# Three of 31 convolution steps moved to GpSimd, and four projection rows moved earlier, in the first mixer of a two-layer hybrid block

## The reference, cut to what matters

```python
u = h @ w_in                                        # h: 768 tokens (256 context, 512 latent) x 1024
a = u[..., :CONV_W] * jax.nn.sigmoid(u[..., CONV_W:2 * CONV_W])
bp = u[..., 2 * CONV_W:]
a = dwconv(a, w_dw, b_dw, (15, 15))                 # depthwise, 31 steps; latent rows of 64 tokens apart
a = jax.nn.silu(layernorm(a, ln_g, ln_b))
pooled = stack([centred_mean(bp[g], w) - bp[g] for g, w in enumerate((2, 4, 8, 16))])
p = (einsum('...gc,gcd->...gd', pooled, w_pool) + b_pool) * pool_scale
y = concatenate([a, p], axis=-1) @ w_out            # 2048 rows of w_out: 1024 for a, 1024 for p
```

## Time and profile before

| | |
|---|---|
| median of 3 runs | 2470.08 us |
| the profiled execution | 2473.15 us, of which the span from first to last instruction is 2471.5 us |
| busy in the span | PE 2326.1 us (94%), DVE 1627.3 (66%), ACT 946.7 (38%), POOL 430.7 (17%) |
| mean granted TensorE clock | 0.969 of full speed |
| chain that ended last | PE 78%, DMA 12%, DVE 4% |
| DVE, line 2491 | 232 instructions, 241.1 us |

### The profile page before, as it was taken

The page is one execution under the profiler, slowest core; times in us unless marked ns, Lnnn a source line. Parts: engine busy times, 40 slices in busy tenths (PEclk is TensorE's granted clock), DMA queues, the critical chain, the costliest instruction groups (busy, mean ns, idle before and its releaser), DMA issues.

```text
span 2471.5 us, 42712 instructions
## 1 busy us (share of the span) xinstructions
PE 2326.1 (94%) x16387; PEld 1555.0 (63%) x16388; DVE 1627.3 (66%) x2005; ACT 946.7 (38%) x1167; POOL 430.7 (17%) x461
## 2 busy tenths in 40 slices
PE   5999989998999999999979999999999799999984
PEld 2555534457788888888857887666645455555542
DVE  2799985447888888888876651677534533454544
ACT  3000014115777777777754232466421111111111
POOL 0533531220000000000020000211000223233322
PEclk9999989999999999999979999999998899999997
DMA  9102075529999999999992133212533989999997
GB/s 340 57 33 70 34 287 167 185 112 400 421 422 394 393 388 383 386 391 388 354 353 81 60 126 109 79 56 77 194 147 158 389 319 373 402 421 420 419 420 295
DMA packets 154320, 649.12 MB, mean 263 GB/s; under 512 B 27866, under 2 KB 42874, under 8 KB 99458
## 3 DMA queue, kind: packets, MB, share of 16 engines
q1 hardware_dynamic: 126912, 578.45, 59.5%
q0 software_dynamic: 16192, 57.53, 6.4%
q10 hardware_dynamic: 11138, 12.07, 1.4%
HBM read 595.13 MB, written 52.86 MB: 262 GB/s over the span
## 4 chain that ended last, share of the span: by engine, by line
PE 78%; DMA 12%; DVE 4%; issue 2%; ACT 2%; POOL 1%; SPq 1%; DVEq 0%; ACTq 0%; POOLq 0%
PE ps L968 75%; DMA arena<-in_w_dram 6%; DMA xs_d<-arena 2%; DMA chunk<-in_w_ada_dram 1%; DVE arena L2369 1%; PE ps L1210 1%; ACT arena L1614 1%; PE ps L1188 1%; PE ps L1194 1%; DMA wx<-in_w_dram 1%; DMA arena<-h_d,uix 1%; PE ps L1057 0%; POOL arena L767 0%; DMA buf_d<-arena 0%; DVE arena L2146 0%
## 5 line engine op out<-in xcount | busy, mean ns | idle before, releaser
L968 PE MATMUL ps<-arena 128*32 128x256 f32 (+5 forms) x10296 | 1192.7, 409 | 37.7 <-ACT arena L1614 10.9
L968 PEld LDWEIGHTS ps<-arena 128*32 128x32 f32 (+1 forms) x10296 | 652.8, 130 | 523.8 <-issue 320.7
L2422 DVE TENSOR_TENSOR wl<-wx,wh 128x2048 fp32r<-128x2048 f32 x228 | 511.5, 2285 | 25.2 <-ACT wh L1614 25.2
L1614 ACT ACTIVATE arena<-ps 128x256 f32<-128x256 f32 (+5 forms) x389 | 176.6, 478 | 863.4 <-PE ps L968 624.9
L1614 ACT ACTIVATE wh<-wx 128x2048 fp32r<-128x2048 f32 x228 | 432.6, 1915 | 85.1 <-PE ps L968 73.0
L2369 DVE COPY arena<-arena 128x2048 f32<-128x2048 f32 x180 | 222.8, 1297 | 274.0 <-PE ps L968 231.7
L968 PE MATMUL ps<-wh,xT 128*128 128x512 f32 x1184 | 380.4, 395 | 6.6 <-DVE xT L2428 4.2
L968 PEld LDWEIGHTS ps<-wh,xT 128*128 128x128 f32 x1184 | 223.2, 188 | 59.2 <-DVE xT L2428 4.6
L2491 DVE SCALAR_TENSOR_TENSOR arena<-arena,par 128x768 f32<-128x768 f32 x232 | 241.1, 1112 | 0.0
L968 PE MATMUL ps<-wl,xT 128*128 128x512 f32 x608 | 239.9, 395 | 0.0
L968 PE MATMUL ps<-wh,gT 128*128 128x512 f32 x608 | 199.5, 399 | 0.0
(11 more groups left out here) (362 smaller groups left out, 2270.5 us busy)
## 6 DMA issues: line engine op xcount, KB each, us to landing
wx<-in_w_dram SPq DMA_DIRECT2D x228, 1024.0 KB, 8.6
arena<-in_w_dram SPq DMA_DIRECT2D x192, 1024.0 KB
arena<-in_w_ada_dram SPq DMA_DIRECT2D x40, 1024.0 KB, 8.8
craw<-in_w_in_c_dram SPq DMA_DIRECT2D x8, 2048.0 KB, 9.0
buf_d<-arena POOLq DMA_DIRECT2D x1, 14848.0 KB, 57.3
arena<-buf_d POOLq DMA_DIRECT2D x19, 512.0 KB, 10.7
buf_d<-arena POOLq DMA_DIRECT2D x19, 512.0 KB, 7.9
arena<-in_w_in_ab_dram SPq DMA_DIRECT2D x8, 1024.0 KB, 12.5
```

Of the source, the lines that this page charges most:

```text
L968: return pe.matmul(bank_ap, lhsT, rhs, start=first, stop=last)
L1614: return act.activation(out_, in_, f, **kw)
L2422: v.tensor_tensor(wl[:, g], wx[:, g], whs[g % NH].bitcast(F32), ALU.subtract).then_inc(m["low"], 1)
```

## The change

For each tile, POOL takes the last three steps of the convolution (28, 29 and 30), after its pooling work for the tile of the same number and after DVE has laid out the padded input: three tensor_scalar and two adds of 768 elements, into an accumulator `gacc`. DVE does 28 steps, adds its two accumulators, waits for POOL, and adds `gacc`. The four rows of `pooled_half(1, ...)` that stood between the two `group_sums` are taken out one by one into the list, as steps h0 to h3. They need banks 6 and 7 for themselves from h0 on, so p5 to p7 use banks 1 and 2, and the modulation vectors 0 to 2 share bank 0, for which slices s4 and s8 wait until ACT has copied the vector before.

```diff
+        gacc = [at(o, S) for o in (6144 + 12 * S, 6144 + 13 * S) * 3 + (49616, 49616 + S)]
...
                 assert n == POOL_DONE[p]
+                pool.wait_ge(conv_s, CONV_OPS * p + 2)
+                acc = gacc[p].rearrange("p (r w) -> p r w", w=GRID_W)
+                for k in range(VTAPS, TAPS):
+                    src, w = apad[p % 2][:, :, k:k + GRID_W], par[:, p, k:k + 1]
+                    if k == VTAPS:
+                        step(pool.tensor_scalar(acc, src, w, None, ALU.mult))
+                    else:
+                        part = at(40912, ROWS, GRID_W)
+                        step(pool.tensor_scalar(part, src, w, None, ALU.mult))
+                        step(pool.tensor_tensor(acc, acc, part, ALU.add))
...
                 if kind == "mods":
+                    if i in (4, 8):
+                        pe.wait_ge(u_ev, i // 4)
                     mods(i)
+                    continue
+                if kind == "half":
+                    for half in range(2):
+                        pe.wait_ge(wo_in[2 * half + 1], 16)
+                    pe.wait_ge(p_rdy, i + 1)
+                    pooled_half(1, lambda k, t: catT[:, k, t * P:(t + 1) * P], wo, KD + i, KD + i + 1)
                     continue
...
             group_sums(lambda ct: catT[:, ct, :], range(4))
-            pooled_half(1, mixed, wo, KD, KD + 4)
             pe.wait_ge(conv_s, CONV_OPS * KD)
...
                 if kind == "pooled":
                     act.wait_ge(pg_mm, i + 1)
+                    if i in (4, 5):
+                        act.wait_ge(conv_s, CONV_OPS * (i + 1))
...
-                for k in range(TAPS):
+                for k in range(VTAPS):
...
-                v.wait_ge(conv_s, CONV_OPS * ct + 2 + TAPS)
+                v.wait_ge(conv_s, CONV_OPS * ct + 2 + VTAPS)
                 v.tensor_tensor(acc[0], acc[0], acc[1], ALU.add).then_inc(conv_s, 1)
+                v.wait_ge(conv_s, CONV_OPS * ct + 3 + VTAPS)
+                v.wait_ge(pool_s, POOL_DONE[ct] + GTAPS)
+                v.tensor_tensor(catT[:, ct, :], catT[:, ct, :], gacc[ct], ALU.add).then_inc(conv_s, 1)
...
-VBANK = (0, 1, 2, 3, 0, 2, 0, 6, 0, 2)
+VBANK = (0, 0, 0, 3, 0, 2, 0, 6, 0, 2)
+VCOL = (0, 256, 0, 0, 0, 0, 0, 0, 0, 0)
...
-CONV_OPS = 2 + TAPS + 1
+VTAPS = 28
+GTAPS = 2 * (TAPS - VTAPS) - 1
+CONV_OPS = 2 + VTAPS + 2
...
-              "s0 s1 p5 s2 s3 s4 s5 s6 p6 s7 s8 s9 p7 s10 s11").split():
+              "s0 s1 p5 s2 s3 h0 h1 s4 s5 s6 h2 p6 s7 h3 s8 s9 p7 s10 s11").split():
```

More of the change, by code:

```diff
@@ L369, in vector_ps @@
         def vector_ps(w, c):
-            return ps[32 * c:32 * c + 2, VBANK[w], 0:UW]
+            o = VCOL[w]
+            return ps[32 * c:32 * c + 2, VBANK[w], o:o + UW]
         vstage = [at(o, UW) for o in (1024, 2048, 3072, 43120, 36976, 37232, 29696, 49520, 48256, 50432)]
@@ L1403, in _ @@
                     pe.wait_ge(pool_s, POOL_DONE[2 * g + 1])
-                    wide(3072, lambda k: wpool[:, 2 * g + k, q * P:(q + 1) * P],
+                    wide(pooled_at(i), lambda k: wpool[:, 2 * g + k, q * P:(q + 1) * P],
                          lambda k: pooled[(2 * g + k) % 4], 2).then_inc(pg_mm, 1)
@@ L1630, in vector_out @@
                 act.wait_ge(u_mm, 4 * w + 4)
-                go(vstage[w], ps[:, VBANK[w], 0:UW], ACT.Copy).then_inc(u_ev, 1)
+                go(vstage[w], ps[:, VBANK[w], VCOL[w]:VCOL[w] + UW], ACT.Copy).then_inc(u_ev, 1)
                 if ST_OF[w] is not None and w != 6:
@@ L1891, in _ @@
                     act.wait_ge(pg_mm, i + 1)
-                    go(catT[:, KD + i, :], psf[:, 3072:3072 + S], ACT.Identity,
+                    if i in (4, 5):
+                        act.wait_ge(conv_s, CONV_OPS * (i + 1))
+                    b0 = pooled_at(i)
+                    go(catT[:, KD + i, :], psf[:, b0:b0 + S], ACT.Identity,
                        scale=par[:, i, TAPS + 4:TAPS + 5], bias=pscb[:, i:i + 1]).then_inc(p_rdy, 1)
@@ L2726, in x_sem, with pooled_at @@
     return x_place(n, j) % 3
+def pooled_at(i):
+    return 512 if i >= 5 else 3072
 def lg_before(n, t):
@@ L2830 @@
 for _p in range(KD):
-    POOL_DONE.append((POOL_DONE[-1] if _p else 0) + (2 * (_p // 2 + 1) + 4 if _p < 6 else 11))
+    POOL_DONE.append((POOL_DONE[-1] + GTAPS if _p else 0) + (2 * (_p // 2 + 1) + 4 if _p < 6 else 11))
 AB_ORDER, _last = [], None
 for _step in ("V0 G0 P0 V1 G1 P1 V2 G2 P2 V3 p0 G3 P3 V4 p1 G4 P4 V5 G5 P5 V6 p2 G6 p3 V7 P6 G7 p4 P7 "
-              "s0 s1 p5 s2 s3 s4 s5 s6 p6 s7 s8 s9 p7 s10 s11").split():
-    _kind = {"V": "value", "G": "gate", "P": "pool", "p": "pooled", "s": "mods"}[_step[0]]
+              "s0 s1 p5 s2 s3 h0 h1 s4 s5 s6 h2 p6 s7 h3 s8 s9 p7 s10 s11").split():
+    _kind = {"V": "value", "G": "gate", "P": "pool", "p": "pooled", "s": "mods", "h": "half"}[_step[0]]
     AB_ORDER.append((_kind, int(_step[1:]), _last))
```

## The result

The changed kernel takes 2512.42 us (median of 3 runs, 2511.96 to 2513.47) against 2470.08, +42.3 us by the medians. The ratio of the two is put at 1.0166 with a 95% interval of 1.0151 to 1.0182, which is +41.0 us (37 to 45). The forecast was 2503.1 with a range of 2488 to 2524. The profiled execution took 2513.47 with a span of 2511.8, 40.3 more than the span before; it lies 1.0 above the median of its runs, where that of before lay 3.1 above, so the two spans differ by 40.3 and the two medians by 42.3.

The account below looks back on a forecast made before the run. DVE's convolution chain, lengthened by POOL's turns, was to bound: its end +32.2 us (-13.9 +10.8 -3.2 +38.5), the second sum +30.4, clock +2.6, total +33.0, median 2503.1 us; 8-in-10 range 2488 to 2524.

Parts of the forecast that it names:

- Two chains, and which one decides: Ahead of the second sum: PE's rows (361.45) and DVE's blocks (359.53) end almost together; both must shorten to win.
- PE's idle time: Ahead of the second sum: PE idle for about 30 us, with a lowered clock behind it.
- The price of a turn: DVE's steps beside POOL: a tensor_scalar takes out 0.65 us, an add 1.54, a tile's five instructions 5.0.
- Held or in turns: Per tile: 5.0 us if POOL gets its turns, 6.3 if held until DVE's pause; 5.5 taken for tiles 1 to 7.
- The condition that I gave: POOL's instruction coming just after a DVE step started is held until DVE's next pause.
- what block 1 gets back: Block 1 of the convolution: tile 0's pooling instructions no longer disturb it, which gives back 3.2 us.
- Tile 0: the step that failed: Ahead of tile 0's last add: POOL's held pooling and five new instructions make DVE wait 10.8 us.
- Slack and the idle time of V7: V7 has 13.5 us of room; tile 5 about 25 us later, V7 about 10, slices end near 360, costing nothing more.
- Behind the second sum: After some 30 us of idleness PE runs at a lowered clock and nothing hides it: +2.6 us, once.
- The distance from that sum to the end: From the second sum to the kernel's end: unchanged within 3 us.

Follow-up runs that it names:

- experiment 1: Changed kernel with the moved rows and shared banks only, all 31 steps on DVE and none on POOL: 2473.62 us, ratio 1.0011 to the kernel before.
- experiment 3: Changed kernel with the last three steps left out altogether, 28 on DVE, none on POOL, rows moved: 2460.41 us, ratio 0.9956 to the kernel before.
- Experiment 4: Changed kernel with all 31 steps of tile 0 kept on DVE, POOL beginning with tile 1: 2499.56 us, ratio 1.0121 to the kernel before.
- experiment 2: Changed kernel with the three steps on POOL but the four rows, banks and order as before: 2509.49 us, ratio 1.0157 to the kernel before.
- Experiment 5: Kernel before, plus three tensor_scalars of 768 elements on POOL in each of tiles 0 to 6, into unread scratch: 2490.24 us, ratio 1.0079.
- experiment 7: Changed kernel with 32 projection multiplies moved ahead of the second sum: 2504.11 us, ratio 1.0132 to the kernel before.
- experiment 6: Kernel before, plus two adds of 768 elements on POOL in each of tiles 0 to 6, into unread scratch: 2490.35 us, ratio 1.0074.
- experiment 8: Changed kernel, steps off POOL, first two steps per tile on ACT, 29 on DVE, next tile's product earlier: 2465.28 us, ratio 0.997 to the kernel before.

## Why the prediction was right, and where it was mis-sized

**Two chains, and which one decides.** Right. PE has 20.89 us of idle time ahead of the second sum and DVE none behind tile 0; the moved rows alone give 1.0011, and 24 steps less on DVE at no price give 0.9956. PE's idle time is 9 us less than the 30 forecast, mostly because the slices ended later (below). What the moved rows give PE was set too low: 350.8 instead of 354.3 for its arrival (experiment 1), so there were 11 us to win on PE's side (experiment 3) and not 7.

**The price of a turn.** Right: 0.65 for a tensor_scalar and 1.56 for an add (forecast 0.65 and 1.54), so 3 x 0.65 + 2 x 1.56 = 5.07 for a tile's five against 5.0. For the tensor_scalar this is luck: the figure is right by a reason that does not hold. I took 0.65 as the instruction's own 0.9 less 0.25. It lasts 2.21, and what it takes out of DVE is a fraction of that. The Trainium skill (SBUF — State Buffer, Who interferes with whom) has two-input VectorE instructions contend with GpSimd's reads, over a port pair that it calls an exclusive lock. The rows of the add look like that (the step at 132.03 lasts 2.56 us, until after the add's end at 133.78), the rows of the tensor_scalar don't: the step at 131.10 starts 0.58 us before the tensor_scalar of 129.25 ends (131.68), and takes the usual 1.00 us.

**Held or in turns.** Half wrong. I expected the first new instruction to be held until DVE's pause in some tiles, at 6.3 a tile. In none of tiles 1 to 7 does DVE wait in front of line 2519. The waits view shows that POOL was ready before the release in four tiles, and even there it got its turn (40 us of waiting for DVE's edge copies, in 4 waits of at most 11.8):

```profile
POOL arena L801 <- DVE arena L2503: 39.7, 4, 11.8
```

The condition that I gave, a start just after that of a DVE step, does not hold either. It fits the kernel before: the add at 84.31, held for 21.42 us, came 0.23 us after the start of a step, the one at 115.33, not held, 0.32 us after. With the change an add that came 0.43 us after a step's start (146.44) was held for 10.33 us, and one that came 0.04 us after (179.99) was not.

Tiles 1 to 7 with what block 1 gets back: forecast -12.2 - 3.2 + 38.5 = +23.1, measured +21.2. With 5.07 in each tile and no 6.3 the sum is -12.2 - 3.2 + 35.5 = +20.1; the last 1.1 us I can't assign.

**Tile 0: the step that failed.** Its wait was forecast at 10.8 us and is 15.36. The sum behind it had three tensor_scalars at 0.9; alone they last 2.21, which is 3 x 1.31 = 3.9 of the 4.6. I had bounded the operation by the memset and the add, 0.70 to 1.8, and the truth lies outside both. One duration stood for two quantities: how long it holds DVE's step, and how long DVE waits for its result. Only the second enters in tile 0: -2.80 for the steps, +15.36, +2.06 for the add is the +14.6 measured, where the terms of the forecast make 9.1. The add itself is 1.0 of the difference: a pooling add of POOL starts at 119.25, and it lasts 2.06 us instead of 0.96. Experiment 4 gives some 12.8 us of the 14.6 back.

**Slack and the idle time of V7.** The mechanism is right, its size not: tile 5's product starts 31.4 us later (285.92) where I had 25, V7 waits 15.9 us for it (the row at 286.94) and starts some 17 us late instead of 10, and the slices end at 372.5 instead of the 360 forecast. None of it shows in the end, since 372.5 still lies ahead of 395.5.

**Behind the second sum.** Forecast +2.6, measured +6.2 (40.3 - 34.1): 2.0 up to the projection, from the clock (2.79 and 4.44 against 1.50 and 3.70). The distance from that sum to the end was to be unchanged within 3 us; it is not. Then 1.5 at 450.48, where PE waits 2.42 us instead of 0.94. POOL and DVE meet here too. The two in that place, after and then before:

```profile
444.69 6.35 POOL L815 TENSOR_TENSOR arena<-cst,arena 128x128 f32<-128x128 f32 x12
...
445.19 3.90 DVE L2188 SCALAR_TENSOR_TENSOR arena<-arena,rs 128x1024 f32<-128x1024 f32 x1
```

```profile
409.03 2.42 DVE L2166 SCALAR_TENSOR_TENSOR arena<-arena,rs 128x1024 f32<-128x1024 f32 x1
```

It is not one turn but the reverse of POOL's being held. With nothing of POOL beside it an instruction of this kind and size takes 1.23 us (line 2146, 435.51); here eight of POOL's twelve short multiplies run back to back before the next one is held in its turn, in the kernel before only four. The instruction takes 3.9 with the change and in experiments 2, 4, 5 and 7, and 2.4 in 1, 3, 6 and 8. Experiment 5 has none of the changed steps, so they are not needed for it; what decides how many of POOL's multiplies run first I can't say. The rest of some 2.7 us is spread over what follows: four multiplies right behind take 3.13 instead of 1.88, the eight of line 1069 ahead of them 1.66 instead of 1.23, and the distance between equal matmuls of the two traces goes up and down by 1 to 2 us to the end. What makes each of these I did not pursue.

Together: the convolution +36.0 (forecast +32.2), the sum +34.1 (+30.4), the span +40.3 (+33.0). The miss of 7.3 us is made of errors of both signs: tile 0 was 5.6 us too low, tiles 1 to 7 were 1.9 too high, and what follows the second sum was 3.6 too low.

## What to carry to other kernels

Work given to GpSimd beside a VectorE chain that bounds has two prices, and they are read from different rows: what it takes out of the steps beside it (the pitch of their starts, here 0.65 to 1.56 us) and how late its result is (its duration alone, here 1.8 to 2.2 us). Add them up per tile against what is taken away before the work is moved; here 5.1 us of turns and a 1.0 us add bought 2.8 us. An engine that takes no such turns is the better taker: ScalarE, mostly idle here, took two steps a tile, and the kernel became 7.4 us faster than before (together with the moved rows and the earlier product, which I did not try apart from it; how much of the 7.4 is ScalarE's is not shown). And where another engine's finish stands 2 us behind, the most that any of it can bring is small: some 11 us with the three steps gone for nothing and the rows moved.

## What the runs showed of the hardware

- GpSimd's tensor_scalar with a factor per partition takes longer than its two-input add: 2.21 against 1.81 us for 768 fp32 elements, with no other engine in its way. It takes less out of a VectorE step: 0.66 against 1.24 us as a mean of 21 and 14.
- A GpSimd instruction that meets VectorE in the middle of a dense row of steps is sometimes held for the whole row (18.63 us, here across the rest of 26 steps; 21.42 in the earlier trace rows). This happened to pooling adds only, to the first after a pause of POOL each time; none of the 35 new instructions of tiles 1 to 7 lasted more than 3.81 us. What decides it I can't say.
- The reverse occurs too: an instruction of VectorE over 1024 elements lasted 3.90 us beside twelve short multiplies of GpSimd, 2.42 in the kernel before, 1.23 with nobody beside it.
- 6.96, 8.19, 14.63 and 20.89 us of idleness of PE all lead to the same 2.79 us for the 16 multiplies of the sum instead of 1.50. The eight multiplies behind it take 3.81 to 4.81 us instead of 3.70 (4.81 after 8.19 us, 3.81 after 14.63, 4.44 after 20.89), so the whole price does not go by the length of the pause. In the stretch with the longest of them the granted clock is 0.64.
- The pause just ahead does not tell the clock by itself. After 0.70 us the first sum takes 1.50 us with the change (373.20) and in experiments 1 and 2, but 2.79 in the kernel before, behind the pauses of 3.35 and 2.24 us of the earlier trace rows as well, with a granted clock of 0.50 from 351.7 to 354.3:

```profile
351.66 2.79 PE L968 MATMUL ps<-arena,ones 128*32 128x512 f32 x16 [0.70 <-ACT arena L1614]
```
